# A new beginning for a two-block layer in float32 parts: vectors, p and mixing weights laid out by partition, x scaled by rows and then turned, two transfer queues in another order

## What is computed

```python
h = rmsnorm(x, norm_g)                       # x * rsqrt(mean(x*x)+1e-6) * norm_g
proj = h @ w_in + b_in                       # 1024 x 8192
u, v, za, ab, ab_gate, zb, g_a, g_b = split(proj)
y_a = gelu(u) * (masked a_ws mix of normalized gelu(v) + a_bs) * silu(za)
y_b = silu(groupnorm(conv31(ab * sigmoid(ab_gate)))) * silu(zb)
merged = sigmoid(g_a) * (y_a @ w_pa) + sigmoid(g_b) * (y_b @ w_pb)
x = x + merged @ w_out
x = x + sigmoid(rmsnorm(x) @ w_ple_gate) * (p @ w_ple)
# the second block: two attentions, a gated recurrence, a squared-relu MLP, a last rmsnorm
```

## Time and profile before

| | |
|---|---|
| median of 3 runs | 795.05 us (793.85 to 795.46) |
| the profiled execution, its own time | 793.99 us |
| its span in the trace | 792.0 us |
| TensorE busy | 765.4 us, 97% of the span, 5604 matmuls |
| DVE, ACT, POOL busy | 554.9, 394.1, 176.0 us |
| mean granted TensorE clock | 0.984 of full speed |

### The profile page before, as it was taken

The page is one execution under the profiler, slowest core; times in us unless marked ns, Lnnn a source line. Parts: engine busy times, 40 slices in busy tenths (PEclk is TensorE's granted clock), DMA queues, the critical chain, the costliest instruction groups (busy, mean ns, idle before and its releaser), DMA issues.

```text
span 792.0 us, 13560 instructions
## 1 busy us (share of the span) xinstructions
PE 765.4 (97%) x5604; PEld 719.7 (91%) x5604; DVE 554.9 (70%) x887; ACT 394.1 (50%) x473; POOL 176.0 (22%) x107
## 2 busy tenths in 40 slices
PE   5999999999999999998999999999999999999996
PEld 4998999999999999887999999999999888888884
DVE  4694693999865776986899775665776656655664
ACT  4645354454645355752484545555346543544442
POOL 2798587974000001410002310000000000000000
PEclk8999999999999999998999999999999999999998
DMA  8765454556354569464354665544645654566521
GB/s 266 236 178 173 141 162 149 160 159 213 126 195 148 171 235 297 122 212 146 122 160 153 207 179 168 158 157 148 217 137 186 208 186 164 183 212 208 167 102 53
DMA packets 118543, 137.86 MB, mean 174 GB/s; under 512 B 4624, under 2 KB 109400, under 8 KB 118489
## 3 DMA queue, kind: packets, MB, share of 16 engines
q1 hardware_dynamic: 118009, 135.52, 53.2%
q0 software_dynamic: 480, 1.57, 0.8%
HBM read 132.88 MB, written 4.19 MB: 173 GB/s over the span
## 4 chain that ended last, share of the span: by engine, by line
PE 81%; DVE 10%; DMA 3%; ACT 2%; issue 1%; POOL 1%; SPq 1%; DVEq 0%; ACTq 0%
PE sums L1460 17%; PE sums L1461 16%; PE sums L1462 16%; PE sums L1832 7%; PE misc L1848 4%; PE misc L1850 4%; PE misc L1851 4%; PE sums L1834 4%; DVE s_wlo L849 2%; DVE sums L914 2%; DMA bias_by_distance<-s_reg_s 1%; ACT s_whi L512 1%; DMA s_raw<-in_w_ple_gate 1%; PE sums L1495 1%; PE sums L1497 1%
## 5 line engine op out<-in xcount | busy, mean ns | idle before, releaser
L512 ACT ACTIVATE s_whi<-s_raw 128x2048 fp32r<-128x2048 f32 (+2 forms) x94 | 176.1, 1875 | 61.0 <-PE sums L1462 36.9
L849 DVE TENSOR_TENSOR s_wlo<-s_raw,s_whi 128x2048 fp32r<-128x2048 f32 (+1 forms) x69 | 157.5, 2284 | 67.8 <-ACT s_whi L512 67.6
L1460 PE MATMUL sums<-s_a_parts,s_whi 128*128 128x256 f32 x576 | 164.5, 286 | 2.4 <-DVE s_wlo L849 2.4
L1461 PE MATMUL sums<-s_a_parts,s_whi 128*128 128x256 f32 x576 | 163.7, 284 | 0.0
L1462 PE MATMUL sums<-s_a_parts,s_wlo 128*128 128x256 f32 x576 | 163.6, 284 | 0.0
L1460 PE MATMUL sums<-s_b_hi,s_whi 128*128 128x256 f32 (+1 forms) x536 | 155.7, 291 | 0.3 <-DVE s_reg_d L1015 0.3
L1461 PE MATMUL sums<-s_b_lo,s_whi 128*128 128x256 f32 (+1 forms) x536 | 153.0, 286 | 0.0
L1462 PE MATMUL sums<-s_b_hi,s_wlo 128*128 128x256 f32 (+1 forms) x536 | 152.9, 285 | 0.0
L437 POOL TENSOR_TENSOR s_wlo<-s_raw,s_whi 128x1024 fp32r<-128x1024 f32 x53 | 130.6, 2486 | 39.9 <-ACT s_whi L512 39.7
L1460 PEld LDWEIGHTS sums<-s_a_parts,s_whi 128*128 128x128 f32 x576 | 111.2, 193 | 3.7 <-DVE s_wlo L849 2.9
L1461 PEld LDWEIGHTS sums<-s_a_parts,s_whi 128*128 128x128 f32 x576 | 111.3, 193 | 0.0
(11 more groups left out here) (314 smaller groups left out, 1306.4 us busy)
## 6 DMA issues: line engine op xcount, KB each, us to landing
s_raw<-in_w_in SPq DMA_DIRECT2D x62, 1024.0 KB, 5.7
s_raw<-in_w_up SPq DMA_DIRECT2D x16, 1024.0 KB, 5.5
s_raw<-in_w_down SPq DMA_DIRECT2D x16, 1024.0 KB, 6.6
s_raw<-in_w_pa SPq DMA_DIRECT2D x6, 1024.0 KB, 5.4
s_raw<-in_w_pb SPq DMA_DIRECT2D x6, 1024.0 KB, 5.4
s_raw<-in_w_out SPq DMA_DIRECT2D x4, 1024.0 KB, 5.1
s_raw<-in_w_ple_gate SPq DMA_DIRECT2D x4, 1024.0 KB, 6.7
s_raw<-in_w_o SPq DMA_DIRECT2D x4, 1024.0 KB, 5.1
```

The source lines that it names most:

```text
L512: act.activation(ring_view(whi, c), ring_view(raw, c), ACT.Copy).then_inc(Sm["hi_ready"], 1)
L849: ve.tensor_tensor(dst, src, part.bitcast(F32), ALU.subtract).then_inc(Sm["lo_ready"], 1)
L1460: pe.matmul(dst, sh, mh, start=first and k == 0, stop=False)
L1461: pe.matmul(dst, sh, ml, start=False, stop=False)
```

## The change

What is laid out by the host instead of the chip: one array `vectors` (128 partitions, 480 columns) with all vectors by partition, x turned (`x_T`), p turned (`p_T`) and `a_ws` turned (`ws_T`). x itself is loaded as before.

What stands in the first steps: ACT squares the first half of x's rows and DVE the second; DVE multiplies x by its row factor while rows are still partitions (`xr`); TensorE turns `xr` instead of x; ACT takes `norm_g` as the scale of its copy from PSUM into `a_hi`; DVE makes `a_lo` from PSUM in one step. The spread row factor, the vector transposes and copies, the turning of p and `a_ws`, and the copies into `xT` are gone. Unit 0 is loaded and rounded in two halves, and POOL has no share in its `lo`. `hi` of unit 1 stands on ACT between the fourth and the fifth tile.

```diff
 def shared(c):
-    return c < SHARED_END and UNITS[c][0] not in ("ki", "ple", "ple2")
+    return 0 < c < SHARED_END and UNITS[c][0] not in ("ki", "ple", "ple2")
...
 # SP
+                if c == 0:
+                    sy.dma_start(dst[:, 0:KD // 2, :], src[:, 0:KD // 2, :]).then_inc(Sm["first_loaded"], 16)
+                    dst, src = dst[:, KD // 2:, :], src[:, KD // 2:, :]
+                sy.dma_start(dst, src).then_inc(loaded[c % SLOTS], 16)
...
-                if c == 0:
-                    for tile, r0, src in vector_loads:
-                        sy.dma_start(vec_rows[r0:r0 + src.shape[0], tile, :], src
-                                     ).then_inc(Sm["vec2_loaded" if tile else "vec_loaded"], 16)
-                if c == 1:
-                    sy.dma_start(ws_rows, I["a_ws"][0].rearrange("g i j -> i g j")).then_inc(Sm["early_loaded"], 16)
+                if c == 2:
+                    sy.dma_start(vectors[:, 120:], I["vectors"][:, 120:]).then_inc(Sm["vec2_loaded"], 16)
+                    sy.dma_start(wsT, I["ws_T"]).then_inc(Sm["early_loaded"], 16)
                     sy.dma_start(bs_bc, I["a_bs"][0].partition_broadcast(P)).then_inc(Sm["early_loaded"], 16)
                     sy.dma_start(bias_v, I["b_in"][:, 1024:2048]).then_inc(Sm["early_loaded"], 16)
-                    sy.dma_start(p_rows, I["p"][0, 0].rearrange("(r p) k -> p r k", p=P)
-                                 ).then_inc(Sm["early_loaded"], 16)
+                    sy.dma_start(pT_raw, I["p_T"]).then_inc(Sm["early_loaded"], 16)
+                if c == 6:
+                    sy.dma_start(xT[:, :, :], I["x_T"]).then_inc(Sm["xT_loaded"], 16)
...
 # ACT
+            act.dma_start(vec, I["vectors"][:, 0:120]).then_inc(Sm["vec_loaded"], 16)
             act.wait_ge(Sm["consts"], 9)
...
-            hi(0)
+            act.wait_ge(Sm["first_loaded"], 16)
+            act.activation(whi[:, 0, 0:UW // 2], raw[:, 0, 0:UW // 2], ACT.Copy).then_inc(Sm["first_hi"], 1)
+            act.wait_ge(loaded[0], 16)
+            act.activation(whi[:, 0, UW // 2:], raw[:, 0, UW // 2:], ACT.Copy).then_inc(Sm["hi_ready"], 1)
+            act.wait_ge(Sm["vec_loaded"], 16)
             for k in range(KD):
-                act.wait_ge(Sm["xn_ready"], k + 1)
-                act.activation(a_hi[:, k, :], xn[:, k, :], ACT.Copy).then_inc(Sm["in_hi"], 1)
-            hi(1)
+                if k < 4:
+                    act.wait_ge(Sm["xr_T"], k + 1)
+                else:
+                    act.wait_ge(Sm["in_lo"], k - 3)
+                act.activation(a_hi[:, k, :], M[k % 4][:, S * (k // 4):S * (k // 4) + S], ACT.Copy,
+                               scale=vec[:, C_NORM + k:C_NORM + k + 1]).then_inc(Sm["in_hi"], 1)
+                if k == 3:
+                    hi(1)
...
 # DVE
+            ve.wait_ge(Sm["x_loaded1"], 16)
+            link(ve.tensor_tensor_reduce(out=abc[:, 2 * UW + D:3 * UW], in0=x_rows[:, 1, :], in1=x_rows[:, 1, :],
+                                         scale=1.0, scalar=0.0, op0=ALU.mult, op1=ALU.add, accum_out=ssq[:, 1:2]))
...
             for r in range(NR):
+                ve.tensor_scalar(xr[:, r, :], x_rows[:, r, :], rstd[:, r:r + 1], None, ALU.mult
+                                 ).then_inc(Sm["xr_ready"], 1)
...
+            ve.wait_ge(Sm["first_hi"], 1)
+            first_lo(0, "first_lo")
+            ve.wait_ge(Sm["vec_loaded"], 16)
+            for k in range(KD):
                 if k == 2:
+                    ve.wait_ge(Sm["hi_ready"], 1)
+                    first_lo(1, "lo_ready")
+                ve.wait_ge(Sm["in_hi"], k + 1)
+                ve.scalar_tensor_tensor(a_lo[:, k, :], M[k % 4][:, S * (k // 4):S * (k // 4) + S], col(vec, C_NORM + k),
+                                        a_hi[:, k, :].bitcast(F32), ALU.mult, ALU.subtract
+                                        ).then_inc(Sm["in_lo"], 1)
             lo(1)
...
 # TensorE
             for r in range(NR):
+                pe.wait_ge(Sm["xr_ready"], r + 1)
+                for k in (0, 4, 1, 5, 2, 6, 3, 7):
+                    at = S * (k // 4) + P * r
+                    ins = rows_T(xr, k, r, M[k % 4][:, at:at + P])
+                    if r == NR - 1 and k >= 4:
+                        ins.then_inc(Sm["xr_T"], 1)
```

More of the change, by code:

```diff
@@ L569, in _ @@
                 if c == 1:
[L570 removed]
+                    act.wait_ge(Sm["vec2_loaded"], 16)
                 if kind == "ab":
@@ L1485, in columns, with arriving @@
                 ins.then_inc(Sm["multiplied"], 1)
-            def arriving(units, h, l, arrive, early=6, between=None):
+            def arriving(units, h, l, arrive, early=6, between=None, begin=begin):
                 def tile_products(c, k):
@@ L1910 @@
     arrays = {f"in_{n}": np.ascontiguousarray(inputs[n]) for n in _INS}
+    arrays["in_vectors"] = np.ascontiguousarray(np.concatenate([inputs[n].reshape(-1, P) for n in _VECTORS]).T)
+    arrays["in_x_T"] = by_partition(inputs["x"][0].T)
+    arrays["in_p_T"] = by_partition(inputs["p"][0, 0].T)
+    arrays["in_ws_T"] = np.ascontiguousarray(inputs["a_ws"][0].transpose(2, 0, 1))
     arrays["onehot"] = distance_buckets()
@@ L1916 @@
     out = nc.dram_tensor("out", [1, S, D], F32, kind="ExternalOutput").ap()
-    block_program(nc, {n: aps[f"in_{n}"] for n in _INS}, aps["onehot"], aps["causal"], scratch, out)
+    block_program(nc, {n[3:]: a for n, a in aps.items() if n.startswith("in_")}, aps["onehot"], aps["causal"], scratch, out)
     r = run_bass_kernel_spmd(nc, [arrays], core_ids=[0])
```

150 lines of the change are left out of this document (38 added, 112 removed).

## The result

The changed kernel takes 784.25 us as the median of four runs (784.05 to 784.83), the kernel before, run beside it, 794.54 (793.85 to 795.46): a ratio of 0.9871, 95% interval 0.9854 to 0.9888. The profiled execution took 784.26 us, 9.7 less than the 793.99 of before, with a span of 782.5 us against 792.0. The forecast was 788.2 with a range from 785.7 to 791.0. The direction was right, the size was too small.

The account below looks back on a forecast made before the run. TensorE, busy 97% of the span, was taken as the bound, so its unbroken run's start counts. Gains 6.0 + 0.9 = 6.9 us off 793.99 gave 787.1, plus 1.06 for the median 788.2; range 785.7 to 791.0.

Parts of the forecast that it names:

- unit 1 earlier: At the beginning: TensorE starts unit 1 at 19.2 us instead of 25.39, 6.2 us earlier.
- change of that until unit 5: Units 1 to 5: POOL's `lo` and gating leave 6.0 us of the 6.2 at unit 5.
- transposes of `a_ws`: Between units 5 and 6: eight TensorE transposes go, 1.04 us busy, 0.9 in distance between starts.
- median above the profiled execution: Whole kernel: the median lies 1.06 us above the profiled execution, turning 787.1 into 788.2.
- scatter: Later in the trace: a fall to half clock costs up to 1.7 us; the shifted run may have one more or less.
- the early case: Rival with unit 1's transfer there before 12.7 us: gain 8.0 us, time 787.0, chance 0.14.
- Unit 1's rounding: On ACT behind tiles 0 to 3: waits for unit 1's transfer, runs from 13.7 to 15.6 us.
- transfers are earlier than ACT needs them: Rival: unit 1 landed before 12.7, starting at 18.3; 787.0 us if unit 3 comes before 23; chance 0.14.
- Squares, scaling, turning: First steps: DVE's square 1.2 us, two scalings 0.8 each, 16 transposes from 8.7 to 12.3.
- Tiles 0 to 3, and the halves of unit 0: Unit 0: tiles' `lo` done at 14.3; extra halves hidden under the transposes, about 1 us if not.
- `lo` of unit 1: Before unit 1: POOL from 15.6 to 18.0, DVE 1.1 us behind it, done at 19.1.
- The supply: Units 3 to 5: unit 3 lands at 24.0, ready 30.7 against demand 30.8; 6.0 of 6.2 us left.

Follow-up runs that it names:

- the 2.38 us step above: DVE's `a_lo` of one tile beside POOL's piece, in the changed kernel with the row factor spread over columns again; that run measured 791.14 us, ratio 0.9969.
- The extra megabyte: Changed kernel with one more 1.05 MB transfer behind unit 2 in SP's queue, unread until much later: 790.01 us, ratio 0.9946.
- the filled wait: Changed kernel with 40 unread products before TensorE's 5.3 us wait for DVE at L1728: 783.29 us, and 782.6 us when run again.
- the one shifted by 16 products: Changed kernel with 16 more unread products of 256 columns behind unit 5: 787.8 us, ratio 0.9927.
- the spread products: Changed kernel with the eight 4-row products between two units spread in pairs over the next unit's first half: 787.62 us, ratio 0.9914.

## Why the forecast fell short

The forecast was 3.9 us too high. By the two traces this splits as follows:

| term, us | forecast | measured | part of the miss |
|---|---|---|---|
| unit 1 earlier | 6.2 | 6.75 | 0.55 |
| change of that until unit 5 | -0.2 | +0.11 | 0.3 |
| transposes of `a_ws` | 0.9 | 0.80 | -0.1 |
| fall of the clock near 190 | 0 | 1.47 | 1.5 |
| unit 6 to 27, unit 47 and the end | 0 | 0.6 | 0.6 |
| median above the profiled execution | +1.06 | -0.01 | 1.1 |

Three steps of the prediction failed, the clock's fall the largest.

**The fall of the clock.** It was put under "scatter" and stood with nothing in the sum; it came on the side of the gain, with 1.5 us. The low end of the range took the early case "less a fall's share"; the whole 1.7 off 787.0 would have given 785.3.

**The median.** I took the change's median to be 1.06 us above its profiled execution, as it was in three runs of the kernel before. No row speaks for that: it was their scatter (in the five later sets the kernel before has medians of 793.4 to 793.8, below its profiled 793.99). In the change the two are 784.25 and 784.26. Without this addition the same sum gives 787.1. Without it and with the whole fall the range would have begun at about 784.3, beside the measured 784.25.

**Unit 1's rounding.** I took 13.7 from the transfer. It landed at 12.09, and ACT came to it at 12.99. I had left unit 0's landing at today's 10.1, and it came at 9.08, 1.0 of the 1.6 us; unit 1 took 3.0 us behind it instead of 3.6, the other 0.6. The 332 GB/s of the earlier trace rows alone were not far off (351 from 9.0 to 12.1 us, 375 from 12.7 to 19.4). The prediction also reads the old trace wrongly where it says that the stream from 2 to 27 us has no pause: from 9.2 to 10.2 it moved 51 GB/s, as unit 1 was issued at 9.23 behind the small loads. The rival "transfers are earlier than ACT needs them" had this right, at 0.14, and its condition (unit 1 there before 12.7, unit 3 before 23; it landed at 21.8) is what the trace shows. It named 18.3 for unit 1, against 18.64 measured and my 19.2. The rule of the Trainium skill's page "DMA: Bandwidth & Descriptors", section "Anatomy of one DMA", gave about 10.1 for unit 1 as an estimate: earlier than my 13.7, as the landing was, and 2 us too early.

What held:

**Squares, scaling, turning.** DVE's square took 1.23 us (I took 1.2), the two scalings 1.41 together (1.6), the turning began at 8.93 and took 3.65 (8.7 and 3.6).

**Tiles 0 to 3, and the halves of unit 0.** "The extra halves cost nothing" is right, and "without it, they would cost about 1 us" is too low: without them and with POOL's share unit 1 comes 3.6 us later.

**`lo` of unit 1.** POOL's 2.42 us, and DVE's end 1.07 behind POOL's (17.40 and 18.47), as the 1.1 of the forecast. The explanation, that the two do not work at the same time, is borne out by the 2.38 us step above; and where DVE began first, POOL's piece took 3.39. **The clock** rose at 13.5, six products into unit 0, before the 16 that I had set as its bound.

**The supply.** I took 0.2 off for POOL; nothing was lost (6.86 at unit 5 against 6.75 at unit 1). Unit 3 landed 2.2 us before my 24.0. The extra megabyte shows that this step was rightly asked: there are 1.6 us of slack and no more.

**Is that fall scatter?** Partly settled. For scatter: the fall at 232 (later in the slower kernels) is in 17 of the twenty traces and missing in three, one of them the filled wait, whose second trace has it. Times of one kernel stand in groups: 786.27, 786.33, then 787.8, 787.94, then 789.65 for the one shifted by 16 products. And the mean granted clock, which is on record for every execution, differs within one kernel: 0.988 to 0.993 in twelve executions of the change, where the one at 0.988 is the slowest (785.59), and 0.983 to 0.993 in 68 of the kernel before. A fall is 0.002 of it, so single executions differ by one and more; in the kernel before the time does not follow it closely (792.2 and 794.2 both occur at 0.993). Against: the fall at 190 is in all six traces in which unit 1 began at 22.2 or later, and in none of the thirteen in which it began at 20.7 or earlier (the spread products left out). Neither the time at which the short products run nor a half clock at the start explains it, by the runs above. What does stays open; so 1.5 of the 9.7 us are shown as the clock's, and not shown as the change's merit or luck.

Nor is such a fall always worth its 1.5 us. Of the two traces of the filled wait one has no fall at 232. TensorE gains 1.48 us by it there and is 1.0 ahead of the other trace behind 236; at unit 47, which waits for the chain behind the bias table's store, the two stand at 309.72 and 309.82.

## What to carry to other kernels

Price a transfer queue by when its entries are issued, not by bytes and rate alone: eighteen small loads of 0.22 MB together took SP 7 us to issue and cost the megabyte behind them 3.9 us. When a chain has two ways to the same product (here ACT's tiles and a transfer), shortening one gives only the distance to the other. The long wait of TensorE cost its length and then the half clock behind it; 40 unread products in it gave 1.8 us back. Do not carry the scatter of three runs into a forecast as a constant.
